# A second pair of PSUM banks for the indexer's scores, relus ahead of q's turning copies, and q's last rope sum behind the choice of keys

## What is computed

```python
bq = rope(parts["b_q"].reshape(b, s, B_HEADS, B_HD), positions)
bk = rope(parts["b_k"].reshape(b, s, B_KV_HEADS, B_HD), positions)
iq = rope(parts["i_q"].reshape(b, s, IDX_HEADS, IDX_HD), positions)
ik = rope(parts["i_k"][:, :, None, :], positions)[:, :, 0, :]
...
rel = jax.nn.relu(jnp.einsum("bthd,bsd->bths", qi_b.astype(jnp.float32), kif))
score = jnp.einsum("bth,bths->bts", wi_b.astype(jnp.float32), rel)
score = jnp.where(key_pos < limit, score, -jnp.inf)
_, sel = lax.top_k(score, topk)
```

## Time and profile before

| | |
|---|---|
| median of 3 runs | 869.52 us (869.16 to 870.04) |
| the profiled execution: its own time | 868.51 us |
| its span from first to last instruction | 866.7 us |
| mean granted TensorE clock | 0.993 |
| PE busy | 839.8 us, 97% of the span |
| DVE busy | 492.6 us, 57% |
| ACT busy | 467.8 us, 54% |
| POOL busy | 474.6 us, 55% |

### The profile page before, as it was taken

How to read it: one execution, slowest core, us unless ns; L and a number is a source line. 1 busy time by engine, 2 the same in 40 slices (tenths; PEclk the granted TensorE clock), 3 DMA queues, 4 the chain that set the end, 5 groups by cost and what they waited for, 6 DMA issues and landing times.

```text
span 866.7 us, 16357 instructions
## 1 busy us (share of the span) xinstructions
PE 839.8 (97%) x6313; PEld 752.2 (87%) x6313; DVE 492.6 (57%) x994; ACT 467.8 (54%) x740; POOL 474.6 (55%) x372
## 2 busy tenths in 40 slices
PE   8999999999999999889899999999999999999995
PEld 7989888999999998679899998999889888888883
DVE  3642144772322327653497825345467699999983
ACT  5455254644534556863348433234455577878763
POOL 5978765989989887677754442355778000000000
PEclk9999999999999999999999999999999999999998
DMA  8644434446555453454722212222544679999931
GB/s 318 214 190 147 162 115 155 177 169 219 194 194 194 164 183 141 145 180 140 231 99 98 98 62 88 98 101 98 189 149 164 269 299 360 355 380 347 357 140 48
DMA packets 24141, 160.98 MB, mean 186 GB/s; under 512 B 3200, under 2 KB 3728, under 8 KB 5392
## 3 DMA queue, kind: packets, MB, share of 16 engines
q1 hardware_dynamic: 21456, 154.67, 49.0%
q10 hardware_dynamic: 2624, 5.44, 1.9%
HBM read 157.62 MB, written 1.05 MB: 183 GB/s over the span
## 4 chain that ended last, share of the span: by engine, by line
PE 86%; DVE 8%; ACT 3%; issue 1%; DMA 1%; POOL 1%; ACTq 0%; SPq 0%; DVEq 0%
PE bank L1150 72%; PE bank L1682 3%; PE bank L1894 1%; PE bank L2011 1%; DMA raw<-weights_dram 1%; PE bank L1344 1%; DVE work L2466 1%; DVE bank L2526 1%; POOL w_lo L586 1%; PE bank L1248 1%; PE bank L1308 1%; PE bank L1296 0%; DVE best L2525 0%; DVE work L2499 0%; PE bank L1711 0%
## 5 line engine op out<-in xcount | busy, mean ns | idle before, releaser
L586 POOL TENSOR_TENSOR w_lo<-raw,w_hi 128x512 fp32r<-128x512 f32 x368 | 474.4, 1327 | 194.2 <-ACT w_hi L627 194.0
L1150 PE MATMUL bank<-h_hi,w_hi 128*128 128x256 f32 x864 | 250.9, 290 | 2.0 <-DVE h_lo L2110 1.4
L1150 PE MATMUL bank<-h_lo,w_hi 128*128 128x256 f32 x864 | 244.8, 283 | 0.0
L1150 PE MATMUL bank<-h_hi,w_lo 128*128 128x256 f32 x864 | 244.7, 283 | 0.0
L627 ACT ACTIVATE w_hi<-raw 128x1024 fp32r<-128x1024 f32 x184 | 188.4, 1058 | 83.3 <-PE bank L1150 50.5
L1150 PEld LDWEIGHTS bank<-h_hi,w_hi 128*128 128x128 f32 x864 | 165.9, 192 | 7.2 <-POOL w_lo L586 2.2
L1150 PEld LDWEIGHTS bank<-h_lo,w_hi 128*128 128x128 f32 x864 | 166.1, 192 | 0.3
L1150 PEld LDWEIGHTS bank<-h_hi,w_lo 128*128 128x128 f32 x864 | 166.0, 192 | 0.0
L1150 PE MATMUL bank<-w_hi,g_hi 128*128 128x512 f32 x208 | 81.6, 392 | 0.0
L1150 PE MATMUL bank<-w_hi,g_lo 128*128 128x512 f32 x208 | 81.1, 390 | 0.0
L1150 PE MATMUL bank<-w_lo,g_hi 128*128 128x512 f32 x208 | 81.0, 390 | 0.0
(11 more groups left out here) (401 smaller groups left out, 1364.0 us busy)
## 6 DMA issues: line engine op xcount, KB each, us to landing
raw<-weights_dram SPq DMA_DIRECT2D x119, 1024.0 KB, 4.8
spare<-weights_dram SPq DMA_DIRECT2D x18, 1024.0 KB, 5.1
tok<-weights_dram SPq DMA_DIRECT2D x9, 1024.0 KB, 4.9
x_sb<-x_dram SPq DMA_DIRECT2D x2, 512.0 KB, 4.3
work<-final_norm_dram ACTq DMA_DIRECT2D x2, 512.0 KB, 4.8
work<-work ACTq DMA_DIRECT2D x8, 128.0 KB, 6.3
work<-constants_dram ACTq DMA_DIRECT2D x1, 640.0 KB, 5.5
con<-constants_dram ACTq DMA_DIRECT2D x1, 520.0 KB, 3.9
```

Source lines behind the costliest of these rows:

```text
L586: ins = nc.gpsimd.tensor_tensor(w_lo[:, part], raw[:, part], w_hi[:, part].bitcast(F32), ALU.subtract)
L1150: ins = mm(dst, a, b, start=start and n == 0, stop=stop and n == 2, skip_group_check=True)
```

## The change

Three things change. The scores of group x = 1 go to banks 6 and 7 (`index_bank`), and PE makes them right behind those of x = 0, ahead of tick 12's quarter; they wait for the values that ACT copied out of bank 6 (`values_stored`). Group x = 2 stays ahead of tick 14's quarter in banks 4 and 5, and waits for the additions of x = 0 alone. ACT takes the relus of x = 0 and x = 1 at tick 12, ahead of the four DMAs that turn the halves of `b_q`, and that of x = 2 at tick 14. DVE adds x = 0 and x = 1 behind one another ahead of the cosines of u = 27, and makes the two sums of `rope(27)` behind `choose_keys`.

```diff
+def index_bank(x):
+
+    return 6 if x == 1 else 4
...
             def index_relu(x):
                 for odd in range(2):
                     act_e.wait_ge(sem("index_scores"), 2 * x + odd + 1)
-                    nc.scalar.activation(bank[4 + odd][:, :], bank[4 + odd][:, :], ACT.Relu).then_inc(sem("index_relu"), 1)
+                    of = bank[index_bank(x) + odd][:, :]
+                    nc.scalar.activation(of, of, ACT.Relu).then_inc(sem("index_relu"), 1)
...
                 delta_slot(2 * tick + 1, delta_step)
+                if tick == 12:
+                    index_relu(0)
+                    index_relu(1)
                 if tick in (4, 8, 12):
                     turn_halves(24 + tick // 4)
-                if tick in (12, 13, 14):
-                    index_relu(tick - 12)
+                if tick == 14:
+                    index_relu(2)
...
-                if x:
-                    pe.wait_ge(sem("index_added"), 4 + 4 * x)
+                if x == 1:
+                    pe.wait_ge(sem("values_stored"), 1)
+                if x == 2:
+                    pe.wait_ge(sem("index_added"), 8)
...
-                if tick in (12, 13, 14):
-                    index_scores(tick - 12)
+                    index_scores(0)
+                    index_scores(1)
+                if tick == 14:
+                    index_scores(2)
...
             index_add(0)
+            index_add(1)
             rope_cosines(27)
-            index_add(1)
-            rope(27, (bq[:, 0:2, :], bq[:, 2:4, :]))
             index_add(2)
             choose_keys()
+            rope(27, (bq[:, 0:2, :], bq[:, 2:4, :]))
             conv2(0, aq, (0,))
```

More of the change, by code:

```diff
@@ L1543, in index_scores @@
                     own = slice(HD * odd, HD * odd + HD)
-                    ins = mm(bank[4 + odd][:, j * keys:(j + 1) * keys], iq[own, h // 2, t * P:(t + 1) * P],
+                    ins = mm(bank[index_bank(x) + odd][:, j * keys:(j + 1) * keys], iq[own, h // 2, t * P:(t + 1) * P],
                              ik[own, 0, 0:keys], start=True, stop=True)
@@ L2490, in index_add @@
                     for j, h in enumerate(heads[odd::2]):
-                        src, w = bank[4 + odd][:, j * keys:(j + 1) * keys], index_w[:, t, h:h + 1]
+                        src, w = bank[index_bank(x) + odd][:, j * keys:(j + 1) * keys], index_w[:, t, h:h + 1]
                         if x < 2 and j == odd == 0:
```

## The result

| | before | changed |
|---|---|---|
| median (range) | 869.34 us (867.32 to 870.04), 6 runs | 875.96 us (874.77 to 890.27), 6 runs |
| ratio, 95% interval | | 1.0074 [1.0059, 1.0089], slower |

0.74% of 869.34 us is 6.4 us; 6.3 us were forecast, and 875.8 us as the time. The profiled execution of the changed kernel (its own time 890.27 us) is one of two disturbed ones of the six, in which PE waits 12.2 us for DVE near 47 us, in code that the change does not touch; medians in this document are over all executions of a kernel, ratios over the undisturbed ones. I therefore read its trace by distances. Everything from the scores of x = 0 on stands 14.98 us later than before (435.73 against 420.75) and I take these 14.98 off where I say "put back".

What follows compares the result with a forecast made beforehand. PE, busy 97% of the span, was taken to bound the kernel. Later tick 16 (+4.7), low clock (+2.0) and time given back (-0.4) sum to +6.3 us on 869.52: 875.8 us, range 873.4 to 878.4.

Steps and rivals of the forecast that it cites:

- tick 16 later than before: PE at tick 16: released by DVE's sums at 445.15 instead of starting at 440.46, 4.7 us later (4.2 to 5.2).
- given back from tick 19 to L1705 (before L1692): PE idles between tick 19 and 500 us, 1.26 us in all, absorb part of the delay: 0.4 us (0 to 1.3).
- forecast's own base: Median of the runs before the change, 869.52 us, to which the forecast added its 6.3 us.
- The gain ahead of tick 16: PE loses its wait for the additions of x = 0; PE and DVE both come 4.8 us earlier.
- The moved sums: DVE's rope(27) sums behind the choice release bank 2 at 445.15; PE stands still 9.5 us ahead of tick 16.
- Rivals 1 and 2: 1: sums do not release tick 16, PE faster, 865.5 us, 3%; 2: gain and loss cancel, 869 to 870 us, 3%.
- Rival 3: Slower but less, 871 to 873.5 us: choice faster without PE writing PSUM beside it, or low clock costs nothing; 8%.
- The clock: PE's clock falls to 1.2 GHz in the wait ahead of tick 16, costing 2.0 us (1.6 to 3.3).
- Rival 4: Slower by more: PE stays at 1.2 GHz through ticks 16 to 18, +12.9 us, 882 us; 4%.
- ACT: At tick 12: four relus to 424.1, then DMAs to 426.6; next weight rounding 1.5 us later, at no cost.

## Why the prediction was right

| step | forecast | traces |
|---|---|---|
| additions of x = 2 begin | 430.5 | 430.44 put back (445.42) |
| sums end, tick 16 is released | 445.1, 445.15 | 445.07, 445.12 put back |
| PE's wait ahead of tick 16 | 9.5 us | 9.38 us |
| tick 16 later than before | +4.7 us | +4.66 us |
| the clock, tick 16 to tick 19 | +2.0 us (1.6 to 3.3) | +2.65 us (11.38 against 8.73) |
| given back from tick 19 to L1705 (before L1692) | -0.4 us | -0.52 us (42.20 against 42.72 from 449.19 to 491.91) |

The last row rests on this row of PE in the kernel before, a wait that both kernels have:

```profile
491.91 1.91 PE L1692 MATMUL bank<-work 64*64 64x64 f32 x64 [0.48 <-DVE work L2612]
```

The three last steps sum to +6.8 us in this one pair of traces, against 6.4 us in the runs. Together with the 14.98 us ahead of them they make 21.77 of the 21.8 us between the spans, 888.5 and 866.7: behind L1705 nothing is gained or lost on the whole.

That the forecast of 875.8 us lies within 0.2 us of the median of 875.96 is luck: without the two executions of 890 us the median is 875.13 us, and the forecast's own base of 869.52 us is 0.18 us above the median of all six runs of the kernel before. What was forecast is the distance, 6.3 us against 6.4 us in the ratio and 6.8 us in the traces.

**The gain ahead of tick 16** was as worked out: the wait of 2.9 us is gone, and both PE and DVE came 4.7 to 4.9 us earlier. The kernels with the banks or the relus alone show this gain, less what PE then still waits, by itself.

**The moved sums** were the step that decided, and three kernels show it: taken back, the loss is a gain of 4 us; alone in the kernel before, they cost 11.4 us (880.93 - 869.57); halfway, the wait is 4.04 us. Rivals 1 and 2 fall with them. Rival 3 gave two causes, and neither came: from 445.42 to 458.77 the choice takes 13.35 us with a PE at rest for most of it, against 13.26 before, and the low clock did cost time.

**The clock** was the term that was sized too low, 2.65 us where I took 2.0, within the bounds. I had sized it by the one fall before, with 3.4 us of work at the low level; here it was 5.85 us. The kernel with 20 matmuls in the wait gives 2.56 us back in its trace. Rival 4 (low through all of ticks 16 to 18) did not come; it was low for 5.85 us of 11.38.

**ACT** was costed wrongly, as if each DMA issue waited for the relus to end. Its timeline in the changed kernel (ACTq are the DMA issues) shows them beside each other:

```profile
436.92 1.07 ACT L901 ACTIVATE bank<-bank 128x512 f32<-128x512 f32 x2 [2.84 <-PE bank L1555]
437.83 0.51 ACTq L878 DMA_DIRECT2D work<-work  x1
437.89 1.08 ACT L901 ACTIVATE bank<-bank 128x512 f32<-128x512 f32 x2
438.38 2.38 ACTq L878 DMA_DIRECT2D work<-work  x3
```

Where the changed kernel is concerned that is without effect, as forecast. In the kernel with two relus ahead the first issue also starts beside the relus (422.34, relus from 422.29 to 423.36), which is part of why it was faster than I expected.

## What to carry to other kernels

Work that is moved behind a long chain takes its release along: before moving an instruction, list everything that waits for its semaphore, not only who needs its result. Here the sums' result was needed at tick 19, but their release of two banks at tick 16, three quarters earlier, and that turned some 4 us of gain into 6 us of loss. And of several edits against one wait, try each alone: two of these three gained some 4 us each, and the third cost over 10 us.

## What was not expected of the hardware

- The low clock lasts longer than one fall showed: PE worked at 1.2 GHz for 3.4 us before, but for 5.85 us behind the wait of 9.38 us. The cost from tick 16 to tick 19 over the 8.73 us of before was 2.65 us there, 2.80 us behind a wait of 4.04 us and 2.33 us (459.60 - 448.54 - 8.73) behind one of 9.29 us, so not ordered by the wait's length. The work at the low level was 5.85, 6.17 and 5.06 us (the granted clock was 0.50 over 454.63 to 460.80 with the sums halfway, and over 448.54 to 453.60 with the sums alone moved).
- The same wait does not always bring the fall. In the kernel with the sums alone moved, PE waited 3.12 us for the scores, longer than the 2.91 us of before, and the granted clock stayed at its high level (windows of PE):

```profile
428.03:432.16 4.13, 4.13 (x32) 1.00 0.55 179
```

- Nor does the same code always keep its clock. Near 364 us PE idles for 0.74 and then 1.57 us, in the seven traces without the early delay to within 0.03 us. In the trace of the sums ahead of the choice the clock fell behind these idles, to 0.52 over 364.50 to 367.50. From the matmul behind the second of them to the next one that waits for DVE's `h_lo`, PE took 9.63 us (364.06 to 373.69), where it took 8.91 us in the kernel before (364.20 to 373.11), whose clock was 1.00 there. The fall cost 0.7 us, and a wait of 0.66 us between the two went away. Of the kernel before, a few executions took 866.8 to 867.3 us where most took 868.7 to 870.3; that the fall near 428 was missing in those would fit, but none of them was profiled.

- A DMA issue on ACT's queue starts while activations ahead of it in the program's order are still to be done: the first at 437.83, before the end of the first pair of relus at 437.99 and before the start of the second pair at 437.89, and the next from 438.38 with these relus running until 438.97.
